# A two-block transformer kernel: layer-norm rows and gather remainders from GpSimd to VectorE, the experts' choice behind the branch, the variances ahead of its end

## The reference

```python
h = layer_norm(x, ln_in_g, ln_in_b)
for l in range(DEPTH):                       # DEPTH = 2
    mix = mixer_sublayer(h, ...)             # proj = h @ w_in; MLA, differential and forgetting attention; o @ w_out
    h = layer_norm(DEEPNORM_ALPHA * h + mix, ln1_g[l], ln1_b[l])
    ffn = grouped_moe(h.reshape(b * seq, d), router_w, router_bias, ...)
    h = layer_norm(DEEPNORM_ALPHA * h + ffn, ln2_g[l], ln2_b[l])
```

## Time and profile before

| | us |
|---|---|
| timed runs, median of 3 | 2431.74 |
| lowest and highest | 2418.53, 2432.99 |
| the profiled execution, its own time | 2426.08 |
| its span, first to last instruction | 2424.3 |
| TensorE busy | 2191.4 (90%) |
| VectorE busy | 1551.8 (64%) |
| ScalarE busy | 1225.5 (51%) |
| GpSimd busy | 101.6 (4%) |

### The profile page before, as it was taken

One profiled execution on the slowest core, in us unless ns is written; L12 is line 12 of the kernel. 1 busy time (PEld: TensorE's weight loads), 2 busy tenths in 40 slices (PEclk: granted clock), 3 DMA queues, 4 the chain that ended last, 5 costly groups with the idle time before them and its releaser, 6 DMA issues.

```text
span 2424.3 us, 32228 instructions
## 1 busy us (share of the span) xinstructions
PE 2191.4 (90%) x12158; PEld 1892.1 (78%) x12158; DVE 1551.8 (64%) x2127; ACT 1225.5 (51%) x1904; POOL 101.6 (4%) x88
## 2 busy tenths in 40 slices
PE   6986999979887999989999887889999998788999
PEld 4765878867676777768998776679989996667998
DVE  7456999975547889976555647555555556555554
ACT  4442777754434777755444443444444444344443
POOL 2001000001001000010000001000000001000000
PEclk9897999988898999989999998899999998789999
DMA  6122899972224999964555432325555554132553
GB/s 218 65 72 88 318 347 357 361 291 92 96 70 142 353 333 347 349 234 158 190 186 180 137 107 82 129 99 182 189 173 174 191 181 169 35 107 87 190 180 117
DMA packets 123926, 447.12 MB, mean 184 GB/s; under 512 B 14544, under 2 KB 15696, under 8 KB 122832
## 3 DMA queue, kind: packets, MB, share of 16 engines
q1 hardware_dynamic: 123760, 444.94, 52.6%
HBM read 443.83 MB, written 1.05 MB: 184 GB/s over the span
## 4 chain that ended last, share of the span: by engine, by line
PE 48%; DVE 5%; ACT 2%; issue 1%; POOL 0%; DVEq 0%; POOLq 0%; ACTq 0%
PE bank L628 7%; PE bank L630 7%; PE bank L629 7%; PE bank L596 4%; PE bank L597 4%; PE bank L598 4%; PE bank L1034 3%; PE bank L1035 3%; PE bank L1036 3%; PE bank L670 2%; PE bank L898 1%; PE bank L2271 1%; DVE lo L559 1%; DVE scr L2883 1%; PE bank L2402 0%
## 5 line engine op out<-in xcount | busy, mean ns | idle before, releaser
L559 DVE TENSOR_TENSOR lo<-stage,hi 128x1024 fp32r<-128x1024 f32 x832 | 977.7, 1211 | 296.5 <-ACT hi L547 277.1
L547 ACT ACTIVATE hi<-stage 128x1024 fp32r<-128x1024 f32 x832 | 842.3, 1044 | 328.2 <-PE bank L598 125.1
L628 PE MATMUL bank<-thi,hi 128*128 128x256 f32 x1504 | 428.1, 285 | 3.3 <-DVE lo L559 2.0
L629 PE MATMUL bank<-tlo,hi 128*128 128x256 f32 x1504 | 427.0, 284 | 0.0
L630 PE MATMUL bank<-thi,lo 128*128 128x256 f32 x1504 | 427.0, 284 | 0.0
L596 PE MATMUL bank<-hi,thi 128*128 128x512 f32 (+2 forms) x656 | 265.7, 405 | 37.5 <-DVE tlo L699 8.5
L628 PEld LDWEIGHTS bank<-thi,hi 128*128 128x128 f32 x1504 | 289.8, 193 | 5.4 <-issue 3.9
L629 PEld LDWEIGHTS bank<-tlo,hi 128*128 128x128 f32 x1504 | 289.7, 193 | 1.4
L630 PEld LDWEIGHTS bank<-thi,lo 128*128 128x128 f32 x1504 | 289.7, 193 | 0.0
L597 PE MATMUL bank<-lo,thi 128*128 128x512 f32 (+2 forms) x656 | 259.5, 396 | 0.0
L598 PE MATMUL bank<-hi,tlo 128*128 128x512 f32 (+2 forms) x656 | 258.9, 395 | 0.0
(11 more groups left out here) (325 smaller groups left out, 2888.4 us busy)
## 6 DMA issues: line engine op xcount, KB each, us to landing
stage<-in_exp SPq DMA_DIRECT2D x384, 512.0 KB, 5.9
stage<-in_ffn SPq DMA_DIRECT2D x264, 512.0 KB, 4.7
stage<-in_wi_a SPq DMA_DIRECT2D x16, 512.0 KB, 6.9
stage<-in_wi_b SPq DMA_DIRECT2D x16, 512.0 KB, 5.1
stage<-in_mem_wkv SPq DMA_DIRECT2D x16, 512.0 KB, 5.4
stage<-in_xwq SPq DMA_DIRECT2D x16, 512.0 KB, 4.3
stage<-in_xwo SPq DMA_DIRECT2D x16, 512.0 KB, 4.5
stage<-in_ssd_xbc SPq DMA_DIRECT2D x12, 512.0 KB, 5.0
```

What stands on the lines that cost most here:

```text
L547: a.activation(self.hi[i % NR][:, x:y], self.stage[(2 * i + p) % (2 * NS)][:, :y - x], ACT.Copy).then_inc(*c.tick(("hi", i, p), sem="hi"))
L559: v.tensor_tensor(self.lo[i % NR][:, x:y], self.stage[(2 * i + p) % (2 * NS)][:, :y - x], self.hi[i % NR][:, x:y].bitcast(F32), ALU.subtra ...
L628: t.matmul(out, hi[:, ws], self.thi[:, xs], start=(k == 0), stop=False)
L629: t.matmul(out, hi[:, ws], self.tlo[:, xs], start=False, stop=False)
```

## The change

GpSimd's `ln_x` in front of both mixers and its gather remainders go to VectorE. In the mixer, VectorE makes the rows of tile 0 after the evacuation of the q heads of the differential attention, and those of tile 1 after the first split of `wi_b`. The source of the layer norm moves to another room, so the copies of the projection no longer wait for the rows; ScalarE waits for them in front of the heads `fq`, whose room overlaps now. Lambda and the rotations stand behind the split of chunk 2 instead of ahead of it, on both engines. In the routing, ScalarE copies tile 0 of X ahead of the sigmoid; VectorE subtracts the gather's remainder of tile 0 behind the groups and that of tile 1 behind the selection matrices; the experts' choice and shares (`gates_dve`) open both bodies of the branch. The variances stand at the end of both bodies, and GpSimd's power waits for `joined` alone.

```diff
-    def ln_pow(self, g, c, S):
+    def ln_pow(self, g, c, S, joined=False):
         for tt in range(2):
             st = self.ln_st(tt)
-            for w in c.need((S, "var", tt)):
+            for w in c.need(None if joined else (S, "var", tt)):
                 g.wait_ge(*w)
@@ begin_pool @@
         self.ln_pow(g, c, "in")
-        for tt in range(2):
-            self.ln_x(g, c, "in", self.room(0, D, 2), tt, "ln_in")
@@ mixer_act (and mixer_dve in the same way with lambda's sums and rotations_dve) @@
-        for w in c.need((S, "lam0")):
-            a.wait_ge(*w)
-        a.activation(self.lam[:, 0:2], self.lam[:, 0:2], ACT.Exp).then_inc(*c.tick((S, "lam1")))
...
         for i, _ in enumerate(proj_in(wi_a, 1024, 0)):
+            if i == 0:
+                for w in c.need((S, "lam0")):
+                    a.wait_ge(*w)
+                a.activation(self.lam[:, 0:2], self.lam[:, 0:2], ACT.Exp).then_inc(*c.tick((S, "lam1")))
...
-                    for x in c.need((S, name, "mm", turn, 0), self.xs(before)):
+                    for x in c.need((S, name, "mm", turn, 0)):
...
-            self.heads_act(a, c, S, "fq", 4, 64, R["fqT"], (6, 7))
+            self.heads_act(a, c, S, "fq", 4, 64, R["fqT"], (6, 7), free=self.xs(before))
@@ mixer_dve @@
             if i == 2:
                 self.heads_dve(v, c, S, "dq", 8, 32, qT, (4, 5, 6, 7), p0=96)
+                self.ln_x(v, c, before, src, 0, "ln_in" if l == 0 else (before, "ln"))
@@ mixer_dve, side @@
             for i, _ in enumerate(proj_in(wi_b, 1024, 1024)):
+                if i == 0:
+                    self.ln_x(v, c, before, src, 1, "ln_in" if l == 0 else (before, "ln"))
@@ moe_rooms @@
-        R["y"] = self.room(2048, D, 2)
+        R["y"] = self.room(2048, D, 2) if l == DEPTH - 1 else self.mixer_rooms()["y"]
@@ moe_act @@
-        for w in c.need((S, "logits")):
-            a.wait_ge(*w)
-        a.activation(R["sc"], self.bank[0][:, 0:32], ACT.Sigmoid).then_inc(*c.tick((S, "sc")))
         for tt in range(2):
             for w in c.need((f"mix{l}", "x", tt)):
                 a.wait_ge(*w)
             a.activation(R["xhi"][tt], self.x(tt), ACT.Copy).then_inc(*c.tick((S, "xhi", tt)))
+            if tt == 0:
+                for w in c.need((S, "logits")):
+                    a.wait_ge(*w)
+                a.activation(R["sc"], self.bank[0][:, 0:32], ACT.Sigmoid).then_inc(*c.tick((S, "sc")))
@@ moe_dve (the 19 instructions of choice and shares move from here to gates_dve) @@
         self.first_max(v, c, mx, grp, top, self.c("c4"), 4)
         c.K.at[S, "grouped"] = c.last
+        def rest(tt):
+            for w in c.need((S, "xhi", tt)):
+                v.wait_ge(*w)
+            v.tensor_tensor(R["xlo"][tt], self.x(tt), R["xhi"][tt].bitcast(F32), ALU.subtract).then_inc(*c.tick((S, "xlo", tt)))
+        rest(0)
...
                                 ALU.is_equal, ALU.mult).then_inc(*c.tick((S, "placed")))
+        rest(1)
         arms(v, c, self.flag[0:1, 0:1], (S, "flag"), lambda: self.compact_dve(v, c, l), lambda: self.dense_dve(v, c, l), S)
         for w in c.need(joined(S)):
             v.wait_ge(*w)
-        for tt in range(2):
-            self.ln_var(v, c, S, tt)
         self.ln_scaled(v, c, S, R["y"])
@@ moe_pool @@
-        for tt in range(2):
-            for w in c.need((S, "xhi", tt), (f"mix{l}", "x", tt)):
-                g.wait_ge(*w)
-            g.tensor_tensor(R["xlo"][tt], self.x(tt), R["xhi"][tt].bitcast(F32), ALU.subtract).then_inc(*c.tick((S, "xlo", tt)))
...
-        self.ln_pow(g, c, S)
-        self.ln_x(g, c, S, R["y"], 0, (S, "ln"))
-        if l < DEPTH - 1:
-            self.ln_x(g, c, S, R["y"], 1, (S, "ln"))
-        else:
+        self.ln_pow(g, c, S, joined=True)
+        if l == DEPTH - 1:
+            self.ln_x(g, c, S, R["y"], 0, (S, "ln"))
             self.rms_x_pool(g, c, "ffn10")
@@ compact_dve @@
+        self.gates_dve(v, c, V, l)
         for k in range(8):
             sl = slice(k * 512, (k + 1) * 512)
...
             for half in range(2):
                 self.ln_stats(v, c, R["y"], tt, half, (V, "sent", 3, tt, half))
+            self.ln_var(v, c, S, tt)
```

More of the change, by code:

```diff
@@ L1513, in proj_in @@
                 if full:
-                    for x in c.need((S, name, "mm", turn, 1), self.xs(before)):
+                    for x in c.need((S, name, "mm", turn, 1)):
                         v.wait_ge(*x)
@@ new lines, in moe_dve @@
+        for w in c.need((S, "places")):
+            v.wait_ge(*w)
+        v.tensor_reduce(cnt[:, 0:1], bk[:, 8:12], AXX, ALU.max).then_inc(*c.tick())
+        for w in c.need(c.last):
+            v.wait_ge(*w)
+        v.tensor_scalar(cnt[:, 0:1], cnt[:, 0:1], 128.0, None, ALU.is_le).then_inc(*c.tick())
+        for w in c.need(c.last):
+            v.wait_ge(*w)
+        v.tensor_copy(self.flag, cnt[:, 0:1]).then_inc(*c.tick((S, "flag")))
+        v.tensor_tensor(g4[:, 0:8], bk[:, 0:8], grp, ALU.mult).then_inc(*c.tick())
@@ new lines, in moe_dve @@
+        for w in c.need(c.last):
+            v.wait_ge(*w)
+        v.tensor_reduce(place, r3(g4[:, 0:8], 4), AXX, ALU.add).then_inc(*c.tick())
+        for w in c.need(c.last):
+            v.wait_ge(*w)
+        v.tensor_scalar(place, place, -1.0, None, ALU.add).then_inc(*c.tick())
+        for w in c.need(c.last):
+            v.wait_ge(*w)
+        for g in range(4):
+            for tt in range(2):
+                i = tt * 4 + g
+                v.tensor_scalar(R["sel"][:, i * 128:(i + 1) * 128], self.c("iota"), place[:, tt:tt + 1], grp[:, i:i + 1],
+                                ALU.is_equal, ALU.mult).then_inc(*c.tick((S, "placed")))
@@ new lines, in moe_dve @@
+        rest(1)
+        arms(v, c, self.flag[0:1, 0:1], (S, "flag"), lambda: self.compact_dve(v, c, l), lambda: self.dense_dve(v, c, l), S)
+        for w in c.need(joined(S)):
+            v.wait_ge(*w)
+        self.ln_scaled(v, c, S, R["y"])
+        if l < DEPTH - 1:
+            c.end(S)
+            return
+        self.turn_dve(v, c, S, "mm", 8, scale="mem_norm")
+        self.ln_x(v, c, S, R["y"], 1, (S, "ln"))
+        for turn, n0, w, full in self.pieces(c, "mem_wkv", D, 2 * D):
+            self.split_dve(v, c)
+            if not full:
+                continue
+            for tt in range(2):
+                if n0 == D and tt == 0:
+                    self.rms_x_dve(v, c, "ffn10", [self.x(0), self.x(1)], R["xn"])
+                if n0 >= D:
+                    for x in c.need((S, "mem_wkv", "mm", turn, tt)):
+                        v.wait_ge(*x)
+                    v.tensor_copy(self.memv[tt][:, n0 - D:n0 - D + w], self.bank[PAIRS[turn % 2][tt]][:, :w]).then_inc(
+                        *c.tick((S, "mem_wkv", "ev", turn, tt)))
@@ L1862, in moe_dve @@
[L1862 to L1879 removed]
+        v.tensor_tensor(r3(oh, 16), r3(t2, 16), bc(mx, 2, 16), ALU.mult).then_inc(*c.tick((V, "gates")))
@@ L1885, in dense_pe @@
         V = (S, "dense")
-        for w in c.need((S, "gates"), (S, "sc")):
+        for w in c.need((V, "gates"), (S, "sc")):
             t.wait_ge(*w)
@@ L1976, in compact_pe @@
             m.then_inc(*c.tick((V, "fetch", k)))
-        for w in c.need((S, "gates"), (V, "xlo", 0)):
+        for w in c.need((V, "gates"), (V, "xlo", 0)):
             t.wait_ge(*w)
```

126 lines of the change are left out of this document (44 added, 82 removed).

## The result

| | before | changed kernel |
|---|---|---|
| timed runs, median (lowest to highest) | 2427.92 (2415.71 to 2442.70), 20 runs | 2405.77 (2396.62 to 2420.19), 20 runs |
| ratio | 1 | 0.9907, 95% interval [0.9885, 0.9929] |
| profiled execution, span | 2424.3 | 2400.5 |
| VectorE, GpSimd busy | 1551.8, 101.6 | 1544.2, 69.5 |

The account below looks back on a forecast made before the run. Expert stages were taken as full, with gains only in serial stretches around them, such as small VectorE instructions before them. Terms 7.5 + 3.8 + 3.15 + 3.8 + 0.25 = 18.5 us, on a base of 2429, gave 2410; range 2399 to 2424.

Parts of the forecast that it names:

- five places: The serial stretches the change could shorten: the kernel's beginning, two routings and two ends of expert stages; 18.5 us in all.
- The start: Layer 0 up to the q heads: they begin at 38.5 instead of 46.15, a gain of 7.5 us, bounds 5 and 9.5.
- The order there: Layer 0: splitting chunk 2 ahead of lambda and rotations ends the third chunk at 36.6, 9.5 us gained if nothing else is late.
- The rows on VectorE at nothing: Mixers: two pairs of row operations each, 9.4 us in all, costed at nothing; without cover at most 2.35 us a pair.
- The routing: Both layers: TensorE's gather starts 4.4 us earlier; 3.8 us taken per layer, bounds 2.4 and 4.4.
- Entering the branch: Routing, VectorE ahead of the expert choices: costs at least nothing and at most 3.16 us, taken nearer to nothing.
- the lower bound: VectorE going into the routing's branch at no cost, so that expert chunk 2's split moves the full 4.4 us.
- The joins: Ends of expert stages 0 and 1: gains of 3.15 and 0.25 us, lower bounds 1.4 and -1.5.
- More than the sum: Rival, chance 0.14: shorter gaps spare clock in four further stretches, 7 us on top, 25 in all, 2404.
- Part is swallowed: Rival, chance 0.20: the weight stream can't restart earlier, both routing terms (7.6 us) go, 10.9 are left, 2418.
- does nothing: Rival, chance 0.07: new waits replace the held-up instructions and the time stays at 2429.

## Why the prediction came out as it did

The time, 2405.8, lies 4 us under the forecast and in the range. The mechanism was right in four of five places; the largest term was wrong, and a gain of granted clock that was not in the sum made up for it. That the total came so near is in part luck.

- **The start: 7.5 forecast, 2.84 measured (4.0 in the mean of seven profiles).** Its first half held: chunk 1 at 2.35, chunk 2 split before TensorE wants it, no gap of 1.00 or 6.79. What failed is the landing of the rows, taken as 4.8 us behind the issue from the kernel before. It took 7.6 us, and 5.4 to 7.6 in the seven profiles of this start. Two things stand beside the load there that the kernel before has not: chunk 2's early split releases a weight load at 24.20, and the two weight loads ahead of it are issued within 1.46 us instead of 3.65. The old order has only the second, and took 6.0 us; the three profiles with GpSimd's rows have neither, and took 4.4 to 4.8. So the second fits all eleven profiles and the first is not needed for them, but no run separates the two, and the cause stays open. The late landing puts the q heads at 40.83, not 38.5. The start's second failure is of kind: the sum let TensorE wait before the q heads and go on at full speed. Behind 4.64 us of idling it runs at a clock of 0.50 for 4 us, which costs 2.49 us more (9.72 against 7.23). 7.65 - 2.33 - 2.49 = 2.83, the measured gain. I had read the same loss of 1.7 us in the gap of the earlier trace rows and not carried it to the new gap.
- **The order there is worth nothing that can be told**, against 9.5 minus waits in the sum: with either order one gap is left, of 4.96 us in the old and 2.2 to 4.7 in the new, and one slow stretch behind it. GpSimd's rows carry the term.
- **The rows on VectorE at nothing: right.** The copy behind them still waits 0.81 us for TensorE.
- **The routing: 2 x 3.8 forecast, 5.38 + 2.18 = 7.56 measured.** On VectorE's path the traces give what was forecast up to the gather, 4.4: two held-up instructions are free (4.0 us), the choices no longer outlast the count (1.7), the second remainder is new (-1.2), in all 4.5 per layer. Undoing the parts one at a time gives 2.7 for the choices' place (and not 1.7, since the first remainder already fills part of the wait for the count) and 0.9 for the remainders' place. Of the 4.0 us, 1.9 are freed already by ScalarE's new order of the copies, as the run with GpSimd's remainders holds up one instruction and not two; no run undoes that order alone. The rest is clock: in layer 0 transposes 0.9 us faster and a gather 0.7 slower; in layer 1 the router's product slower (6.98 us, before 4.89). So the two layers differ by clock, and that 7.56 meets 7.6 is luck: the repeats of the changed kernel give 8.7 and 9.8.
- **Entering the branch: 0.04 us**, so the lower bound held and the split moved 7.6 us, nearly all of the advance in front of it. Leaving it still costs 3.22 and 3.15. The Trainium skill, page "Runtime: NRT & Kernel Launch", section "Instruction fetch mechanics", says that sequential code is fetched ahead and a branch target outside the window is not; both rows agree with it, though no trace shows what fills the 3.2 us.
- **The joins: 3.15 and 0.25 forecast, 3.06 and 0.28 measured.** Undone one by one, the parts of the first are 1.4 (rows) and 0.3 to 0.5 (variances), and the rest goes with either.
- **"More than the sum"** named the granted clock as a gain of about 7 us. The means put it at 9, of which some 4 are the vanished slow stretches themselves, already in the stretches' gains; 5 are left. Its direction was right; its ground, further stretches sped up by shorter gaps, is not shown: why attention 1 and the second block run at one clock or another, no run settles, since one and the same kernel shows both.
- **"Part is swallowed" and "does nothing"** fail at the split: it moved with TensorE, and expert stage 0 took 285.09 and 285.63 us in the first two profiles, before 284.18. Over all 14 profiles it took 281.85 to 289.17 us, with no visible tie to when it began: the earliest of them, at 231.33, took 283.46. So what a later profile lost there is not shown to be lost for having started early.

## What to carry to other kernels

When work is taken from GpSimd, count which VectorE instructions it held up: here taking four row operations from beside the splits was worth 3.7 to 5.2 us, and a carefully moved block nothing that could be told. When a gap is shifted rather than closed, the slow products behind it move along and belong in the sum; and when a step is made earlier, look at the loads that its end releases, since they close up around the one you wait for: its time to landing in the old kernel may not hold in the new (here 4.8 and 7.6 us). Where a part is worth under 5 us in 2400 and the clock wanders, read its stretch between two fixed instructions, and compare the totals at equal granted clock.

## What the hardware showed that I had not expected

- One program, with attention 0 begun at the same 47.18 us, ran the stage in 154.15 or in 166.31 us by granted clocks of 0.91 and 0.84. Attention 1 took from 178.3 to 194.3 us over the profiles here, the window attention from 129.5 to 137.3, with the same products.
- Two remainders of 128x512 took 5.70 us beside GpSimd's row operations and 1.29 without. The Trainium skill, page "SBUF — State Buffer", section "SBUF: two separate sides", describes the port pair of VectorE and GpSimd as an exclusive lock held for the whole instruction; that fits, as each remainder is longer by about 2.2 us, most of one row operation (2.7 to 3.3 us here), and not by a fixed share.
- VectorE makes the same rows in 1.23 us per operation, GpSimd in 2.3 to 3.3.
